# Forming the weight-block sums of a seven-product matrix multiply by loads and accumulating transfers in place of GpSimd arithmetic

## The reference

```python
h2 = _rms(x, p['norm_ffn'])
gt, up = jnp.split(h2 @ p['w_ffn_in'], 2, axis=-1)      # 1024 -> 2 x 2816
x = x + (jax.nn.silu(gt) * up) @ p['w_ffn_out']         # 2816 -> 1024
```

## Time and profile before

| | |
|---|---|
| time of the runs | 2191.19 us median of 3 (2188.92 to 2194.05) |
| the profiled execution, its own time | 2190.47 us |
| its span | 2188.7 us |
| TensorE busy | 2094.1 us, 96% |
| VectorE busy | 1642.8 us, 75% |
| ScalarE busy | 1074.1 us, 49% |
| GpSimd busy | 578.5 us, 26% |
| transfers | 205.96 MB, all issued by SP, 28.3% of the 16 DMA engines |

### The profile page before, as it was taken

How to read it: one execution, slowest core, us unless ns; L and a number is a source line. 1 busy time by engine, 2 the same in 40 slices (tenths; PEclk the granted TensorE clock), 3 DMA queues, 4 the chain that set the end, 5 groups by cost and what they waited for, 6 DMA issues and landing times.

```text
span 2188.7 us, 40099 instructions
## 1 busy us (share of the span) xinstructions
PE 2094.1 (96%) x14428; PEld 1950.3 (89%) x14428; DVE 1642.8 (75%) x3295; ACT 1074.1 (49%) x2379; POOL 578.5 (26%) x427
## 2 busy tenths in 40 slices
PE   8999999999998998999999999999999989989999
PEld 7998868888998898989999987788899978989899
DVE  4467876647669999999745678766575799999995
ACT  4236676566344444444432467665662444444442
POOL 1120020200026454444311200203000354545440
PEclk9999999999999999999999999999999999999999
DMA  5224224142421122222332332241523112212222
GB/s 185 88 90 142 78 93 139 62 143 77 138 93 49 61 85 69 96 70 76 104 102 81 113 113 83 85 146 55 176 76 123 63 58 77 81 60 92 68 94 81
DMA packets 95604, 205.96 MB, mean 94 GB/s; under 512 B 21232, under 2 KB 50544, under 8 KB 95088
## 3 DMA queue, kind: packets, MB, share of 16 engines
q1 hardware_dynamic: 95408, 203.40, 28.3%
HBM read 179.41 MB, written 23.95 MB: 93 GB/s over the span
## 4 chain that ended last, share of the span: by engine, by line
PE 63%; DVE 22%; DVEq 5%; ACT 4%; issue 4%; POOL 1%; DMA 0%; ACTq 0%; SPq 0%
PE ps L1077 14%; DVE op_lo L2729 9%; PE ps L1003 9%; PE ps L1023 7%; PE ps L1089 5%; PE ps L1564 4%; PE ps L1565 4%; PE ps L1566 4%; PE ps L1254 2%; PE ps L1274 2%; PE ps L1150 2%; DVEq L2785 2%; DVE part L2771 1%; DVE a_lo L2757 1%; PE ps L1195 1%
## 5 line engine op out<-in xcount | busy, mean ns | idle before, releaser
L2212 DVE TENSOR_TENSOR w_lo<-raw,w_hi 128x1024 fp32r<-128x1024 f32 (+4 forms) x128 | 145.5, 1136 | 169.4 <-ACT w_hi L1605 164.9
L1077 PE MATMUL ps<-h_hi,w_hi 128*128 128x320 f32 x768 | 246.0, 320 | 0.0
L1077 PE MATMUL ps<-h_hi,w_lo 128*128 128x320 f32 x768 | 237.3, 309 | 0.0
L1077 PE MATMUL ps<-h_lo,w_hi 128*128 128x320 f32 x768 | 237.2, 309 | 0.0
L2157 POOL TENSOR_TENSOR rsq<-ssq,mhalf 128x12 f32<-128x12 f32 (+3 forms) x56 | 117.0, 2089 | 418.5 <-DVE ssq L2324 359.0
L1605 ACT ACTIVATE op_hi<-w_sums 128x512 fp32r<-128x512 f32 (+1 forms) x256 | 148.0, 589 | 155.8 <-PE ps L1566 147.7
L1564 PE MATMUL ps<-th_hi,op_hi 128*128 128x320 f32 x640 | 201.3, 314 | 23.2 <-DVE part L2771 17.7
L1605 ACT ACTIVATE w_hi<-raw 128x1024 fp32r<-128x1024 f32 (+4 forms) x128 | 125.8, 983 | 197.2 <-PE ps L1003 115.1
L2729 DVE TENSOR_TENSOR op_lo<-raw,op_hi 128x512 fp32r<-128x512 f32 (+1 forms) x192 | 208.7, 1088 | 13.9 <-ACT op_hi L1605 13.3
L2729 DVE TENSOR_TENSOR op_lo<-w_sums,op_hi 128x512 fp32r<-128x512 f32 (+1 forms) x256 | 194.7, 762 | 13.7 <-ACT op_hi L1605 0.5
L1566 PE MATMUL ps<-th_hi,op_lo 128*128 128x320 f32 x640 | 199.1, 311 | 0.0
(11 more groups left out here) (411 smaller groups left out, 6135.7 us busy)
## 6 DMA issues: line engine op xcount, KB each, us to landing
raw<-in_weights SPq DMA_DIRECT2D x176, 512.0 KB, 3.5
raw<-in_weights SPq DMA_DIRECT2D x72, 384.0 KB, 3.0
gates<-gst SPq DMA_DIRECT2D x72, 160.0 KB, 1.8
g<-gates SPq DMA_DIRECT2D x12, 960.0 KB, 6.7
ktb<-in_cache_fox_kt SPq DMA_DIRECT2D x16, 384.0 KB, 4.2
vc<-in_cache_fox_v SPq DMA_DIRECT2D x16, 384.0 KB, 3.9
out_y_t<-x_sb SPq DMA_DIRECT2D x12, 320.0 KB, 2.2
raw<-in_weights SPq DMA_DIRECT2D x8, 416.0 KB, 3.0
```

What stands on the lines that cost most here:

```text
L1077: mm = pe.matmul(ps[:, 5, 0:HALF], w[:, kk * P:(kk + 1) * P], h_pair[x][:, kk, half * HALF:(half + 1) * HALF], start=kk == 0 and n == 0, s ...
L2212: return dve.tensor_tensor(low[:, 0:width], raw[raw_slot(c)][:, 0:width], high[:, 0:width].bitcast(F32), ALU.subtract)
```

## The change

The four sums of each seven-product unit are no longer computed by GpSimd. For unit s, SP loads blocks of the weights from memory straight into the four slots of `w_sums` (`begin_sums`, four loads), and GpSimd then issues four transfers that add their source to what lies in the slot: the block (1, 0) of `raw` onto slots 0 and 2, then slot 0 onto slot 1, then slot 1 onto slot 3. GpSimd waits for a transfer to land before it issues one that reads it. All four transfers add, so the sums that had subtractions are formed with other signs, and VectorE's additions of products and activation sums take the signs over: some additions become subtractions, some become one instruction that multiplies by -1 and subtracts, and the one addition to three blocks of an "out" unit becomes two instructions.

`begin_sums(s)` stands in SP's order behind the two chunk loads of unit s + 1.

```diff
-        sums_made, part_made = sig("sums_made", SUMS * len(FAST)), sig("part_made", 5 * len(FAST))
+        sums_begun, sums_begun_late = sig("sums_begun", 16 * 2 * len(FAST)), sig("sums_begun_late", 16 * 2 * len(FAST))
+        sums_first, sums_second, sums_third = (sig(n, w * len(FAST)) for n, w in (("sums_first", 32), ("sums_second", 16), ("sums_third", 16)))
+        part_made = sig("part_made", 5 * len(FAST))
...
                         sp.wait_ge(lo_made.sem, lo_made.at(layer, made_by(s, 5 if k else 4)))
                         own_wait(sp, sp_tick)
-                        sp.wait_ge(sums_made.sem, sums_made.at(layer, SUMS * (s + 1)))
+                        if k:
+                            sp.wait_ge(sums_first.sem, sums_first.at(layer, 32 * (s + 1)))
...
+                def begin_sums(s):
+
+                    c, width = fast_chunk(s), fast_width(s)
+                    def part_of(k, second):
+                        return io["weights"][L, c + k, :, width * second:width * second + width]
+                    if s:
+                        sp.wait_ge(lo_made.sem, lo_made.at(L, max(made_by(s - 1, i) for i in (1, 2, 3))))
+                        own_wait(sp, sp_tick)
+                        sp.wait_ge(sums_second.sem, sums_second.at(L, 16 * s))
+                        own_wait(sp, sp_tick)
+                        sp.wait_ge(sums_third.sem, sums_third.at(L, 16 * s))
+                    else:
+                        sp.wait_ge(w_used.sem, w_used.at(L, USED[C_FF + 1]))
+                    own_wait(sp, sp_tick)
+                    sp.dma_start(w_sums[:, 0, 0:width], part_of(1, 1)).then_inc(sums_begun.sem, 16)
+                    sp.dma_start(w_sums[:, 2, 0:width], part_of(0, 0)).then_inc(sums_begun.sem, 16)
+                    sp.dma_start(w_sums[:, 1, 0:width], part_of(0, 0)).then_inc(sums_begun_late.sem, 16)
+                    if s:
+                        sp.wait_ge(lo_made.sem, lo_made.at(L, made_by(s - 1, 6)))
+                        own_wait(sp, sp_tick)
+                    sp.dma_start(w_sums[:, 3, 0:width], part_of(0, 1)).then_inc(sums_begun_late.sem, 16)
...
                 for c in (C_FF, C_FF + 1, C_O + 6, C_O + 7, *range(C_FF + 2, CHUNKS)):
                     chunk(c)
+                    s = (c - C_FF) // 2 - FF_PLAIN - 1
+                    if c % 2 and 0 <= s < len(FAST):
+                        begin_sums(s)
...
                     if total:
-                        act.wait_ge(sums_made.sem, sums_made.at(L, SUMS * s + total))
+                        if total in (1, 3):
+                            act.wait_ge(sums_first.sem, sums_first.at(L, 32 * (s + 1)))
+                        else:
+                            made = sums_second if total == 2 else sums_third
+                            act.wait_ge(made.sem, made.at(L, 16 * (s + 1)))
...
                 for s in range(len(FAST)):
                     c, width, m = fast_chunk(s), fast_width(s), paired(s - 1) if s else None
-                    for u in range(2):
-                        pool.wait_ge(chunk_landed[raw_slot(c + u)].sem, chunk_landed[raw_slot(c + u)].at(L, 16 * LANDED[c + u]))
-                    if s == 0:
-                        pool.wait_ge(w_used.sem, w_used.at(L, USED[C_FF + 1]))
-                    else:
-                        pool.wait_ge(lo_made.sem, lo_made.at(L, made_by(s - 1, 3)))
-                    pool.tensor_tensor(w_sums[:, 0, 0:width], weight_part(s, 1, 0), weight_part(s, 1, 1), ALU.add).then_inc(sums_made.sem, 1)
-                    pool.drain()
-                    pool.tensor_tensor(w_sums[:, 1, 0:width], w_sums[:, 0, 0:width], weight_part(s, 0, 0), ALU.subtract).then_inc(sums_made.sem, 1)
-                    pool.drain()
-                    pool.tensor_tensor(w_sums[:, 2, 0:width], weight_part(s, 0, 0), weight_part(s, 1, 0), ALU.subtract).then_inc(sums_made.sem, 1)
+                    pool.wait_ge(chunk_landed[raw_slot(c + 1)].sem, chunk_landed[raw_slot(c + 1)].at(L, 16 * LANDED[c + 1]))
+                    pool.wait_ge(sums_begun.sem, sums_begun.at(L, 32 * (s + 1)))
+                    for at in (0, 2):
+                        pool.dma_start(w_sums[:, at, 0:width], weight_part(s, 1, 0), accum_op=ALU.add).then_inc(sums_first.sem, 16)
                     if s == 0:
                         pool.wait_ge(th_made.sem, th_made.at(L, 4))
                         pool.tensor_tensor(th_lo[:, 1, :, :], t_one, th_hi[:, 1, :, :].bitcast(F32), ALU.subtract).then_inc(th_split_too.sem, 1)
-                    else:
-                        pool.wait_ge(lo_made.sem, lo_made.at(L, made_by(s - 1, 6)))
-                    pool.tensor_tensor(w_sums[:, 3, 0:width], weight_part(s, 0, 1), w_sums[:, 1, 0:width], ALU.subtract).then_inc(sums_made.sem, 1)
-                    pool.drain()
+                    pool.wait_ge(sums_begun_late.sem, sums_begun_late.at(L, 32 * (s + 1)))
+                    pool.wait_ge(sums_first.sem, sums_first.at(L, 32 * (s + 1)))
+                    pool.dma_start(w_sums[:, 1, 0:width], w_sums[:, 0, 0:width], accum_op=ALU.add).then_inc(sums_second.sem, 16)
+                    pool.wait_ge(sums_second.sem, sums_second.at(L, 16 * (s + 1)))
+                    pool.dma_start(w_sums[:, 3, 0:width], w_sums[:, 1, 0:width], accum_op=ALU.add).then_inc(sums_third.sem, 16)
...
-                t_sum(a11, a12, a11)
-                t_sum(t_second[:, :, :], a22, a11)
-                t_sum(a21, a21, t_second[:, :, :])
+                t_done(dve.tensor_tensor(a11, a11, a12, ALU.subtract))
+                t_done(dve.scalar_tensor_tensor(t_second[:, :, :], a22, -1.0, a11, ALU.mult, ALU.subtract))
+                t_done(dve.scalar_tensor_tensor(a21, t_second[:, :, :], -1.0, a21, ALU.mult, ALU.subtract))
...
-                                three = x_sb[:, n, second]
-                                three = bass.AP(tensor=three.tensor, offset=three.offset, ap=[list(three.ap[0]), [HALF, 3], [1, HALF]])
-                                dve.tensor_tensor(three, three, rows_bcast(part[0][:, :], 3), ALU.add)
+                                dve.tensor_tensor(column[:, second], column[:, second], part[0][:, :], ALU.add)
+                                dve.tensor_tensor(beside_it.rearrange("p (h n) -> p h n", h=2), beside_it.rearrange("p (h n) -> p h n", h=2),
+                                                  rows_bcast(part[0][:, :], 2), ALU.subtract)
...
                         if i == 2 and kind == "in":
-                            summed(part[1][:, :], part[0][:, :], 2)
+                            negated(part[1][:, :], part[0][:, :], 2)
                             dve.drain()
                         if i == 3 and kind == "in":
-                            summed(part[1][:, :], part[1][:, :], 3)
+                            summed(part[1][:, :], part[1][:, :], 3, ALU.subtract)
```

More of the change, by code:

```diff
@@ L2713, in _, with t_done @@
                 a21, a22 = hx[1][:, 4:KD, first], hx[1][:, 4:KD, second]
-                def t_sum(dst, a, b):
-                    dve.tensor_tensor(dst, a, b, ALU.subtract).then_inc(t_made.sem, 1)
+                def t_done(ins):
+                    ins.then_inc(t_made.sem, 1)
                     dve.drain()
@@ L2745, in pair_total @@
                 def pair_total(m, r):
-                    dst, a, b = ((pair_first(m), ff_act[0][:, second], ff_act[0][:, first]), (ff_act[0][:, second], ff_act[1][:, second], ff_act[0][:, second]),
-                                 (ff_act[0][:, first], ff_act[1][:, second], pair_first(m)), (ff_act[1][:, first], ff_act[1][:, first], ff_act[0][:, first]))[r]
+                    dst, a, b = ((pair_first(m), ff_act[0][:, first], ff_act[0][:, second]), (ff_act[0][:, second], ff_act[1][:, second], ff_act[0][:, second]),
+                                 (ff_act[0][:, first], ff_act[1][:, second], pair_first(m)), (ff_act[1][:, first], ff_act[0][:, first], ff_act[1][:, first]))[r]
                     dve.drain()
-                    dve.tensor_tensor(dst, a, b, ALU.subtract).then_inc(pair_sum.sem, 1)
+                    if r < 2:
+                        last = dve.tensor_tensor(dst, a, b, ALU.subtract)
+                    else:
+                        last = dve.scalar_tensor_tensor(dst, a, -1.0, b, ALU.mult, ALU.subtract)
+                    last.then_inc(pair_sum.sem, 1)
                 def pair_low(m, r):
@@ L2767, in _, with summed, negated @@
                     at = lambda i: ps[:, product_bank(s, i), 0:HALF]
-                    def summed(dst, a, i):
+                    def summed(dst, a, i, op=ALU.add):
                         dve.wait_ge(w_used.sem, w_used.at(L, used_by(s, i)))
-                        return dve.tensor_tensor(dst, a, at(i), ALU.add).then_inc(part_made.sem, 1)
+                        return dve.tensor_tensor(dst, a, at(i), op).then_inc(part_made.sem, 1)
+                    def negated(dst, a, i):
+                        dve.wait_ge(w_used.sem, w_used.at(L, used_by(s, i)))
```

(17 more changed lines are left out.)

## The result

| | before | after |
|---|---|---|
| time of the runs | 2191.08 us, median of 4 (2188.92 to 2194.05) | 2949.52 us, median of 4 (2944.84 to 2953.19) |
| span of the profiled execution | 2188.7 us | 2949.4 us |
| TensorE busy | 2094.1 us, 96% | 2204.7 us, 75% |
| GpSimd busy | 578.5 us, 26% | 445.8 us, 15% |

The kernel is slower: ratio 1.3459, 95% interval 1.3433 to 1.3485. That is +758 us, where +503 was forecast. It lies inside the range of 2460 to 3000 us, in its upper part, and 255 us over the value.

The account below looks back on a forecast made before the run. TensorE or VectorE paced the old kernel; the chain would pace the changed one. D plus high part 1 to low part 5, over 31 steps, gave 634 us a layer against 382: +503 on 2190.5, so 2694 us, range 2460 to 3000.

Parts of the forecast that it names:

- The chain from low part 5: From low part 5 through chunk and sum loads, accumulating pair and slot 1 transfer to high part 1; sets each unit's time.
- D: Length of the chain from low part 5 to high part 1: 14.2 us in "in" units, 12.6 in "out" units.
- From high part 1 to low part 5: Rest of each unit after D: 6.9 us "in" without pair work, 8.9 with it, 5.3 "out".
- The clock term: Product 5 slows after TensorE's gap, matmuls at 0.26 us: adds 0.8 us "in" without pair work, about 0.25 "out".
- The term with pair work: High part 1 to low part 5 in 9 "in" units a layer, slowed entries put at rest times: 8.9 us.
- Two together move 512 KB more: 5.3.: Accumulating pair onto slots 0 and 2, part of D: 5.3 us, or 4.7 with 192 KB blocks.
- 4.8 + 0.1 = 4.9: Start of D: chunk and first two sum blocks, 1024 KB, at 2.2 us + bytes / 400 GB/s; "out" 4.2 us.
- The hop onto slot 1, 4.0: Last transfer in D: 3.5 us plus 0.5 for GpSimd's issue, 4.0 us; 3.7 with 192 KB blocks.
- What costs nothing: GpSimd's and VectorE's savings wait for the chain; fourth load, slot 3 transfer and signs hidden; 24 added instructions, uncovered, 12 us.
- Rival 1: The chain is hidden up to D = 7.2 us ("out" 5.3), TensorE bounds, 24 us less a layer: 2142 us; chance 0.03.
- Rival 2: Cheap hops: accumulates land like plain 256 KB loads, second of a pair free, clock stays up: 2465 us; chance 0.1.
- Rival 3: Dear hops: each takes 7.4 us, a pair 8.7, because issue or adding is slow: 3130 us; chance 0.12.

## Why the prediction was right and wrong

- **The chain and the direction: right.** The chain from low part 5 stands in the trace link by link, and high part 1 is where ScalarE waits, for a transfer. All the time lies in the two stretches. In "out" units the last link is another than foretold: low part 5 waits for high part 5, which waits for product 5.
- **The number: inside the range, and in part by its width.** The range allowed D 5 us over the value, and it came out 3.6 over. Neither main reason for that, the second transfer's wait for room and the gaps around the loads, is named in the prediction.
- **"From high part 1 to low part 5": 6.9, 8.9 and 5.3 us forecast.** In the second layer the means are 7.1 in "in" units without pair work, 10.1 in those with it (mostly 10.3) and 5.7 in "out" units. The clock term held: its 0.26 us is the distance of the last matmuls in the earlier trace rows, and in the changed kernel the matmuls of product 5 stand 0.27 us apart behind the gap, at a granted clock of 0.50 (from 2604.8 to 2608.0). The mean clock of the stretch is 0.76, where it was 0.98. The term with pair work was 1.2 too small, some 9 x 2 x 1.2 = 22 us, and all three together some 34 us, which with D (below) make up the missing 255. The trace shows where that came from: the prediction put all of the pair's low parts at their times at rest, but GpSimd still makes two of its own in these places, and two of VectorE's stand beside them. `h_lo` keeps the 1.16 us that it had, and the first `a_lo` takes 1.23 to 1.49 us in eight of nine units, where others take 0.48 (the line of these low parts in the second stretch; ns, shortest, median and longest):

```profile
L2787 DVE TENSOR_TENSOR h_lo<-ff_act,h_hi x9: 1156/1158/1162, 2165.4 to 2760.6; 128x320 fp32r<-128x320 f32 x9
```

- **The term D: the step that failed.** The sum took 14.2 and 12.6 us; it was 17.9 and 16.1. Over the 62 turns of both layers that is 222 of the missing 255 us. Its pieces:
  - *"Two together move 512 KB more: 5.3."* It was 7.7. The prediction had let the pair run side by side; the second was not even issued until 0.3 us after the first had landed. With 704 the measured pair is 5.6 (4.9 for 384 wide, 4.7 forecast), so the size of the term was nearly right but for this. The term was 145 us short in all; 127 us of the time went with more room, as the run with 704 shows.
  - *"4.8 + 0.1 = 4.9" for the loads.* It was 6.8. The 0.4 us from the two loads behind is shown by the run with half of the loads. The rest is read from the trace and was not tested piece by piece: 0.57 us of issue on SP between the chunk and the first sum load and 0.4 for the second, and 0.6 us from the landing to GpSimd's issue. Queued loads at 400 GB/s say nothing of such gaps. The prediction also left out the unit's first chunk: where it still took over 1 us to land when the first sum load was issued (12 of the 38 turns with 512-wide sums), the loads took 6.8 us from there, and 5.9 in the others. The term was some 120 us short in all.
  - *The hop onto slot 1, 4.0.* It was 3.3 (3.0 for 384 wide), which gives 43 us back. The half microsecond for GpSimd's issue was really 0.87, but it overlaps the landing time that the profile counts from the issue.
- **"What costs nothing": right for the signs,** which are free where they were tried, in the kernel before (1.0005).
- **"A gap of some 7 us before product 5": right in its place, too short.** The waits of TensorE in the second stretch have a mean of 202.3 / 18 = 11.2 us in the "in" units and as much in the "out" units. The longer D accounts for 3.6 us of the difference:

```profile
PE ps L1592 <- DVE part L2805: 202.3, 18, 12.9
PE ps L1592 <- DVE x_sb L2801: 134.9, 12, 13.2
```

- **Rival 1, hidden and faster.** Its price of 2142 us was too modest: with the sums gone TensorE's own gaps go too, and the ceiling is 2116. And the chain was far from hidden: it had 7.2 us to hide in and took 17.9. VectorE does get its time back: 1148 ns became 687. But the most that this could bring was 74 us, and the chain of 62 turns cost 758.
- **Rival 2, cheap hops.** A hop took 3.3 us, not 2.8, and the clock did not stay up: 0.76 in place of 0.98 on the mean of the second stretch.
- **Rival 3, dear hops.** A first hop next to chunk loads does take 5.9 us on the mean, as the run with early loads shows. In the changed kernel none of the chunks was in flight by then, in any of the 64 units.
- **The sign of being wrong that came close.** "If the time per unit is set by GpSimd's issue and not by the landings": the second transfer of a pair is held at its issue, but what lets it go comes 0.3 us behind a landing.

## What to carry to other kernels

Before arithmetic is turned into dependent transfers, count the hops between the event that frees the input and the one that needs the result, and price each as issue, landing and wake-up; here three links (loads, pair, slot 1) of 3 to 8 us stood where 4 us of additions with a unit of lead had been. Ask of each pair of transfers on GpSimd's queue whether the second can be issued at all while the first is under way. And measure the ceiling first: a run with the work left out told that 74 us was all there was to win.

## What was not expected of the hardware

- **Room for GpSimd's transfers.** With `dynamic_dma_scratch_size` at 512 a second accumulate of 256 KB was issued only 2.7 us after the first one's issue had ended, and 5.6 us in the turn shown where that one landed late: 0.3 us after the first had landed, in all 64 units, and so with 8 columns too. With 704 it was issued 2.2 to 4.0 us before the first had landed, and the two issues together took 1.77 us in the turn shown.
- **GpSimd's drain waits for its transfers.** With an accumulate outstanding the time behind the addition was 1.5 to 5.8 us, 3.8 on the mean and 242 us in all, and it ended 0.17 us after the landing in all 64 units; with a wait for the addition's semaphore it was 0.1 us, and the kernel ran 93 us faster.
- **A hop is mostly fixed.** It takes 2.0 us with 8 columns, 3.3 with 256 KB. In the changed kernel 0.6 us more pass from the landing of the pair to GpSimd's next issue, and 0.4 from that of the transfer onto slot 1. Issue takes GpSimd 0.87 us each.
- **Accumulates suffer from company.** 256 KB onto slots 0 and 2 land in 3.3 us in the changed kernel, in 4.2 (median) where the pair runs side by side, and in 6.5 where it runs side by side and beside the chunk loads. Beside the chunk loads alone the first of a pair takes 5.9 on the mean (all widths).
